# Memory keys by heads at four seams, weights split ahead of the rows, an opening and a final norm in another order

## What is computed

```
h = rmsnorm(x, norm_mix_pre[layer])
m = retention_mixer(h, ...)  or  dilated_mixer(h, ...)
x = x + rmsnorm(m, norm_mix_post[layer])
f = conv_ffn(rmsnorm(x, norm_ffn_pre[layer]), ...)
x = x + rmsnorm(f, norm_ffn_post[layer])
```

```
memn = rms_norm(mem, norm_mem)
k = (memn @ wk).reshape(B, M, MEM_HEADS, MEM_HEAD_DIM)
```

## Time and profile before

| | |
|---|---|
| median of three runs | 1215.38 us |
| the profiled execution, its own time | 1215.33 us |
| its span, first to last instruction | 1213.5 us |
| mean granted TensorE clock | 0.999 of full speed |
| busy: PE, DVE, ACT, POOL | 99%, 70%, 57%, 12% |
| HBM read | 208.08 MB, 172 GB/s over the span |
| weight splits on DVE (L2011) | 195, mean 2.19 us |
| weight splits on ACT (L1466) | 195, mean 1.84 us |

### The profile page before, as it was taken

One profiled execution on the slowest core, in us unless ns is written; L12 is line 12 of the kernel. 1 busy time (PEld: TensorE's weight loads), 2 busy tenths in 40 slices (PEclk: granted clock), 3 DMA queues, 4 the chain that ended last, 5 costly groups with the idle time before them and its releaser, 6 DMA issues.

```text
span 1213.5 us, 19309 instructions
## 1 busy us (share of the span) xinstructions
PE 1201.4 (99%) x7660; PEld 1064.7 (88%) x7660; DVE 853.7 (70%) x1235; ACT 694.6 (57%) x1014; POOL 146.5 (12%) x182
## 2 busy tenths in 40 slices
PE   8999999999999999999999999999999999999997
PEld 8888888888888889889888888888999898999896
DVE  5566665866667898888877777677666667566665
ACT  6444335665555755555555656556676567565554
POOL 1000000300001000000001311331101411001500
PEclk9999999999999999999999999999999999999999
DMA  9544434655554445444443755554354453454331
GB/s 368 213 165 173 173 139 156 220 197 195 192 189 165 174 155 169 166 161 157 159 174 122 291 201 179 201 180 173 130 201 140 139 208 110 145 188 137 134 139 53
DMA packets 31992, 210.35 MB, mean 173 GB/s; under 512 B 3665, under 2 KB 3938, under 8 KB 11042
## 3 DMA queue, kind: packets, MB, share of 16 engines
q1 hardware_dynamic: 30258, 202.12, 47.3%
q0 software_dynamic: 1504, 6.76, 1.5%
q10 hardware_dynamic: 144, 0.26, 0.1%
HBM read 208.08 MB, written 1.05 MB: 172 GB/s over the span
## 4 chain that ended last, share of the span: by engine, by line
PE 93%; DVE 3%; ACT 2%; issue 1%; DMA 1%; POOL 0%; SPq 0%; DVEq 0%; ACTq 0%; POOLq 0%
PE pair L757 18%; PE pair L639 15%; PE pair L641 15%; PE pair L640 15%; PE pair L751 10%; PE bank L639 3%; PE bank L640 3%; PE bank L641 3%; PE bank L867 1%; PE bank L1041 1%; PE pair L741 1%; PE bank L1050 1%; DVE wlo L2011 1%; PE bank L1063 1%; ACT whi L1466 1%
## 5 line engine op out<-in xcount | busy, mean ns | idle before, releaser
L2011 DVE TENSOR_TENSOR wlo<-raw,whi 128x2048 fp32r<-128x2048 f32 (+2 forms) x195 | 426.6, 2194 | 152.1 <-ACT whi L1466 151.4
L1466 ACT ACTIVATE whi<-raw 128x2048 fp32r<-128x2048 f32 (+2 forms) x195 | 357.3, 1836 | 167.7 <-PE pair L641 137.8
L757 PE MATMUL pair<-ahl,whi 128*128 128x512 f32 x832 | 208.8, 391 | 0.0
L757 PEld LDWEIGHTS pair<-ahl,whi 128*128 128x128 f32 x832 | 153.1, 188 | 29.4
L639 PE MATMUL pair<-whi,bhl 128*128 128x512 f32 (+3 forms) x416 | 150.7, 362 | 0.0
L641 PE MATMUL pair<-whi,bhl 128*128 128x512 f32 (+3 forms) x416 | 146.0, 351 | 0.0
L640 PE MATMUL pair<-wlo,bhl 128*128 128x512 f32 (+3 forms) x416 | 145.8, 351 | 0.0
L751 PE MATMUL pair<-ahl,wlo 128*128 128x256 f32 x832 | 115.2, 282 | 0.0
L751 PEld LDWEIGHTS pair<-ahl,wlo 128*128 128x128 f32 x832 | 110.5, 191 | 3.9
L639 PE MATMUL pair<-whi,ahl 128*128 128x512 f32 (+3 forms) x288 | 109.0, 379 | 0.0
L641 PE MATMUL pair<-whi,ahl 128*128 128x512 f32 (+3 forms) x288 | 106.0, 368 | 0.0
(11 more groups left out here) (338 smaller groups left out, 1967.4 us busy)
## 6 DMA issues: line engine op xcount, KB each, us to landing
raw<-wstream_d SPq DMA_DIRECT2D x161, 1024.0 KB, 4.8
raw<-wstream_d SPq DMA_DIRECT2D x26, 768.0 KB, 4.5
raw<-wstream_d SPq DMA_DIRECT2D x4, 832.0 KB, 4.9
raw<-wstream_d SPq DMA_DIRECT2D x4, 800.0 KB, 4.4
gain_row<-rows_d POOLq DMA_DIRECT2D x5, 512.0 KB, 4.1
arena<-mem_cols_d POOLq DMA_DIRECT2D x2, 1024.0 KB, 8.0
raw<-wstream_d SPq DMA_DIRECT2D x2, 576.0 KB, 4.0
raw<-wstream_d SPq DMA_DIRECT2D x2, 512.0 KB, 6.2
```

Source lines behind the costliest of these rows:

```text
L757: mm = pe.matmul(pair[:, p, f, :], whi[:, slot, sl], both, start=False, stop=k == KD - 1, skip_group_check=True)
L1466: act.activation(whi[:, n % RING, 0:width[n]], raw[:, n % RAW, 0:width[n]], ACT.Copy).then_inc(hi_ready, 1)
L2011: dve.tensor_tensor(wlo[:, n % RING, 0:width[n]], raw[:, n % RAW, 0:width[n]], whi[:, n % RING, 0:width[n]].bitcast(F32), ALU.subtract).th ...
```

## The change

1. The memory keys of layer 0 are made by heads, one head (a chunk of 128x1024, 24 matmuls) at each of the four seams, in the place of the fillers (`seam_keys`); each result is read out on its own (`read_keys`). The turn of x is cut into these keys: three k-tiles ahead of tile 0, three ahead of tile 1, two behind at seams 1 and 3; seven ahead and one behind at seams 2 and 4. The memory's rows are therefore loaded three times more and their halves made three times more, into whichever row buffer is free there; rows of x wait until the keys have been read from it (`keys_half`, `chunk_used`).
2. Splits of weights stand ahead of the squares and the weighs, or of the rows, in the lists of ACT and DVE.
3. At seams 2 and 4, whose sums lie in banks, all four weighs stand ahead of the update of tile 0.
4. In section 2, layer 0, the factors are spread one place later in the token product.
5. In the opening, the second half of chunk 0 is loaded ahead of the second half of x's columns, and chunk 1 is split in three parts.
6. The gain of the final norm is multiplied in `add_product`, ahead of its wait for PE's last sums.

```diff
-FIRST_PARTS = ((0, 512, 1024, 1536, CW), (0, 1024, CW), (0, 1024, CW))
+FIRST_PARTS = ((0, 512, 1024, 1536, CW), (0, 512, 1024, CW), (0, 1024, CW))
...
+    key_blocks = lambda l, heads: [("block", "mem_wk_2", l, np.concatenate([r(MEM_HD) + h * MEM_HD for h in heads]), r(KD))]
+    blocks += key_blocks(0, SEAM_HEADS[0:1])
...
+    blocks += key_blocks(0, SEAM_HEADS[1:2])
...
-        blocks.append(("block", "mem_wk_2", l, mem, r(KD)))
+        blocks += key_blocks(l, r(MEM_H) if l else SEAM_HEADS[3:4])
...
         mem_rows = cut(4096, NT, D)
-        mem_t = [cut(7000, KD, SEQ), cut(9400, KD, SEQ)]
+        mem_t = [cut(10000, KD, SEQ)] * 3 + [cut(7000, KD, SEQ), cut(9400, KD, SEQ)]
+        mem_rows_of = [(ahi, alo, 0), (bhi, blo, KD)] * 2 + [(bhi, blo, KD)]
...
-                    if c == 0:
-                        sp.dma_start(first_cols[:, FIRST_X[i]:FIRST_X[i + 1]], x_cols_in[:, FIRST_X[i]:FIRST_X[i + 1]]).then_inc(x_cols_sem[i], 16)
+                    if i == 0 and c < 2:
+                        sp.dma_start(first_cols[:, FIRST_X[c]:FIRST_X[c + 1]], x_cols_in[:, FIRST_X[c]:FIRST_X[c + 1]]).then_inc(x_cols_sem[c], 16)
                     sp.dma_start(raw[:, c, a:b], src[:, a:b]).then_inc(w_landed[c] if b == CW else part_in[n], 16)
...
+            pool.wait_ge(x_lo, KD // 2)
+            pool.dma_start(mem_t[0], mem_cols_in).then_inc(mem_in_sem, 16)
...
-            def keep_warm(dst, n):
-
-                for _ in range(n):
-                    pe.transpose(dst, ident[:, :], ident[:, :])
...
+            def seam_keys(seam, *cuts):
+
+                hi, lo, k0 = mem_rows_of[seam]
+                p, c = begin_block("a"), w.chunk
+                slot = c % RING
+                w.chunk += 1
+
+                def some(first, last):
+                    for k in range(first, last):
+                        if k == 0:
+                            pe.wait_ge(lo_ready, c + 1)
+                        if k % 2 == 0:
+                            pe.wait_ge(mem_lo, 4 * seam + k // 2 + 1)
+                        sl = slice(k * MEM_HD, (k + 1) * MEM_HD)
+                        mm = product(pair[:, p, 0, 0:SEQ], whi[:, slot, sl], wlo[:, slot, sl], hi[:, k0 + k, :], lo[:, k0 + k, :], k == 0, k == KD - 1)
+                        if k == KD // 2 - 1:
+                            mm.then_inc(keys_half, 1)
+                        elif k == KD - 1:
+                            mm.then_inc(chunk_used, 1)
+
+                return [lambda a=a, b=b: some(a, b) for a, b in zip((0,) + cuts, cuts + (KD,))]
+
+            def turn_rows(x_there, aside=(nothing, nothing, nothing), held=None):
 
                 base = w.at("turn")
                 for t in range(NT):
...
-                        if k == 0 and filler[t]:
-                            keep_warm(bank[:, 0, t * P:(t + 1) * P] if dst is None else dst, filler[t])
+                        if k == 0:
+                            aside[t]()
                         x_there(t, k)
...
-                if filler[2]:
-                    keep_warm(next_pair(), filler[2])
+                aside[2]()
...
-                turn_rows(added, (4, 9, 0), held=held)
+                turn_rows(added, seam_keys(2 * l, 3, 6), held)
...
-            keep_warm(aside, 18)
-            pe.wait_ge(post_ready, 2 + 4)
             held = []
-            turn_rows(added, (0, 2, 0), aside, held)
+            keys, more, rest = seam_keys(1, 7, 7)
+
+            def sums_weighed():
+                keys()
+                pe.wait_ge(post_ready, 2 + 4)
+
+            turn_rows(added, (sums_weighed, more, rest), held)
...
 
-                ready = []
-
-                def turn_first():
-                    if l == 0:
+                if l == 0:
+                    keys, more, rest = seam_keys(3, 7, 7)
+
+                    def sums_weighed():
+                        keys()
                         pe.wait_ge(post_ready, 2 * (2 + 4))
-                    ready.append(turn_rows(summed if l else added))
-
-                rows_there = lambda a, b: pe.wait_ge(mem_lo, 4 * l + b // 2)
-                features("a", bhi, blo, k0=KD, lhs_ready=rows_there, between=[nothing, nothing, turn_first])
-                ready = ready[0]
-                tokens("v", ahi, alo, lhs_ready=ready, between=[spread_rows])
+
+                    ready = turn_rows(added, (sums_weighed, more, rest))
+                    tokens("v", ahi, alo, lhs_ready=ready, between=[nothing, nothing, spread_rows])
+                else:
+                    ready = []
+                    rows_there = lambda a, b: pe.wait_ge(mem_lo, 4 * 4 + b // 2)
+                    features("a", bhi, blo, k0=KD, lhs_ready=rows_there, between=[nothing, nothing, lambda: ready.append(turn_rows(summed))])
+                    ready = ready[0]
+                    tokens("v", ahi, alo, lhs_ready=ready, between=[spread_rows])
...
+            def rows_out(dst, gain, each=False, classes=False, keys=None):
                 for g in range(KD // 2):
+                    if keys is not None and g == 0:
+                        act.wait_ge(keys_half, keys + 1)
+                    elif keys is not None and g == KD // 4:
+                        act.wait_ge(chunk_used, w.chunk + 1)
...
             def ffn(l):
-                split_hi(w.chunk - 2)
-                rows_out([(ahi, 0)], [COLS["norm_ffn_pre"] + l * KD], True)
+                catch_up()
+                rows_out([(ahi, 0)], [COLS["norm_ffn_pre"] + l * KD], True, keys=2 * l)
+                passed()
+                read_keys(2 * l)
...
+                    if i == FF_TILES - 1:
+                        catch_up()
...
-                row_squares(added if l == 0 else summed)
-
-                catch_up()
-                passed()
+                if l:
+                    row_squares(summed)
+                    catch_up()
+                    passed()
...
+                else:
+                    p, n = read_keys(3)
+                    row_squares(added)
...
+                if not in_pairs:
+                    weigh(1, 0)
+                    weigh(1, 1)
                 dve.wait_ge(post_ready, half_done[0])
                 dve.wait_ge(*done[0])
                 dve.wait_ge(rstd_ready, w.up("rstd"))
                 dve.scalar_tensor_tensor(x[:, 0, :], xn[:, 0, :], rstd[:, 0:1], x[:, 0, :], ALU.mult, ALU.add).then_inc(x_ready, 1)
-                weigh(1, 0)
-                weigh(1, 1)
+                if in_pairs:
+                    weigh(1, 0)
+                    weigh(1, 1)
...
                 dve.tensor_tensor(xh[:, 1, 0, :], xh[:, 1, 0, :], pair[:, p, 0, :], ALU.add).then_inc(x_half, 1)
+                if meanwhile is not None:
+                    meanwhile()
                 w.chunk += 1
                 dve.wait_ge(chunk_used, w.chunk)
                 dve.tensor_tensor(xh[:, 1, 1, :], xh[:, 1, 1, :], pair[:, p, 1, :], ALU.add).then_inc(drained_v[p], 1)
...
+            def final_gain():
+
+                dve.wait_ge(gain_in, 16 * w.up("gain"))
+                dve.wait_ge(x_half, 4 * 3 + 2 * DEPTH)
+                dve.tensor_tensor(xn[:, 1, 0:D // 2], x[:, 1, 0:D // 2], gain_row[:, 0:D // 2], ALU.mult).then_inc(gained, 1)
+
...
+            mem_low(0, 0)
             used(1)
             ret_norm(RET_HEADS - 1, g_at[RET_HEADS - 1])
-            used(2)
+            mem_low(0, 1)
+            used(1)
+            mem_low(0, 2)
+            used(1)
             ret_out(RET_HEADS - 1)
+            mem_low(0, 3)
             used(RET_KT // 2 - 6)
-            passed()
+            used(1)
             add_post(in_pairs=True)
...
+                passed()
+                w.next_block("a")
...
+                    if i >= FF_TILES - KD and i % 2 == 0:
+                        mem_low(2 * l + 1, KD // 2 - (FF_TILES - i) // 2)
...
+            mem_low(2, 0)
+            mem_low(2, 1)
             dil_weigh(c, 1)
...
+            mem_low(2, 2)
+            mem_low(2, 3)
             split_lo(w.chunk - 2)
             dil_osplit(c)
+            catch_up()
             add_post(in_pairs=True)
```

92 lines of the change are left out of this document (53 added, 39 removed).

## The result

Five runs of the change gave 1208.79 to 1209.77 us, median **1209.43**; five of the kernel before 1215.3 to 1215.55, median 1215.35. The ratio is 0.995, 95% interval 0.9939 to 0.996. The forecast was 1209.5.

The account below looks back on a forecast made before the run. PE, busy 99% of the span, was taken to bound the kernel. The terms -1.1 + 1.4 - 0.1 + 1.3 - 7.1 - 0.3 = -5.9 took 1215.33 to 1209.5 us, range 1207.2 to 1213.0.

Parts of the forecast that it names:

- Seam 1: Retention to the first FFN: the up product starts 1.4 us later, with 2.88 of key matmuls inside.
- Seam 2: First FFN to attention: the up product starts 0.1 us sooner, with 2.88 of key matmuls inside.
- Seam 3: Attention to the second FFN: the up product starts 1.3 us later, with 2.88 of key matmuls inside.
- Seam 4: Second FFN to section 2: tokens start 7.1 us sooner, with 8.6 less key work inside and 1.5 of new waiting.
- Tail: End of the kernel: the final gain's product moves into DVE's wait for PE, and 0.3 us reaches the store.
- Signs: If right: next product 5.1 to 5.2 us after PE is free at Seam 1 and Seam 2; DVE wait 1 to 2 at Seam 4.
- Opening: Start of the kernel: PE's two waits for split weights, at 10.60 and 14.44, go; gain 1.1 us.
- The first: Rival at Seam 4: ACT and DVE are quicker and PE loses nothing there; 1208.0 us, chance 0.12.
- The second: Rival at four seams: POOL is held by splits and weighs, each row factor 0.9 us late; 1213.1, chance 0.08.
- The third: Rival behind the seams: weights are split late, a miss of 0.9 us at three seams; 1212.2, chance 0.12.
- The fourth: Rival: DVE's chain sets each seam anyway and keys only fill it; 1213.7 to 1214.5 us, chance 0.07.
- The fifth: Rival at Seam 4 and Seam 2: without fillers TensorE's clock falls; 1218 us and more, chance 0.05.

Follow-up runs that it names:

- experiment 6: The change with DVE's split of the up chunk moved behind tile 0's update at the seams from retention and attention to the FFNs: 1212.18 us.
- experiment 4: The change with tile 1's weighs put back behind tile 0's update, at the seams after the first and second FFN: 1209.17 us.
- experiment 5: The change with the product of the final norm's gain put back behind the last sums: 1210.07 us.
- experiment 3: The kernel before without its 46 filler transposes: 1216.27 us; with only the fillers between first FFN and attention kept: 1215.42 us.
- experiments 2: The change with 14 pairs of warm-up transposes in place of 11: 1209.1 us; the change itself once more: 1209.79 us.
- experiment 7: The change with the token product's first two steps, after the second FFN, doing high-half matmuls before waiting for low halves: 1210.43 us.

## Why the prediction was right, and where it was not

*Seam 1: right, step by step.* The forecast had ACT's split from 199.3 (199.54 measured), DVE's split done at 203.8 (203.85), the weighs done at 205.1 (205.05), tile 0 turned from 206.4 (206.49), the up product at 209.9 (209.87). Part of that is luck: 199.3, 1.9 and 2.29 add up to 203.5, and the 203.8 of the forecast holds 0.3 that it names no row for; ACT began 0.24 late. One bound, "without DVE's delay it would be 209.15", can't be had by moving the split: experiment 6 took it out of the weighs' way and the seam got 1.22 longer. I had looked at what is late for tile 0; the seam ends with tile 1, behind the sum of DVE's work.

*Seam 2: 0.28 sooner, not 0.1.* The chain of the last weigh, x and the turn held (PE waits 0.28, not 0.6). That weighs go first had no part in it, by experiment 4.

*Seam 3: right* (1.36 for 1.3), seam 1 repeated.

*Seam 4: right* (7.08 for 7.1). Of its 6.16, 24 keys take 2.88 and 16 transposes some 1.76; the other 1.5 are the new waiting that was worked out, and the rows name 0.28 of it for x and 0.93 for DVE's low rows.

*Tail: right,* 0.34 for 0.3, and experiment 5 gives back 0.33.

*Signs.* Two of the signs set ahead were just missed: seam 2 took 4.89 and not 5.1 to 5.2, and the wait on DVE at seam 4 was 0.93 and not 1 to 2.

*Opening: this step failed,* the 1.1 of the sum. Its two waits did go, but the pitch of 0.12 on which I valued them was read from one execution. The matmuls of the opening run at 0.21 in others, and with the old order nobody sees it, since PE waits for weights anyway: the kernel before with the slow pace (experiment 3, first profile) reaches the first 512-column matmul at 20.28, with the quick pace at 20.30. The order of the opening removes a wait that hid a slow clock. At the quick pace it is worth 1.36 to 1.45 there and 0.9 to 1.4 at the end (experiments 2, 4 and 5), so the 1.1 was a fair price for that pace; at the slow pace it is worth nothing. The median of five runs holds some of both.

*What made the sum come out:* the FFNs' first up matmuls wait less for high rows (0.12 and 0.14), and section 2 lost 0.33, of which 0.31 lies in one place in its second layer. Before, DVE stands idle for 0.85 ahead of its L2349 at 1109.15, ended by "issue" (nothing that the profile shows), runs 0.3 to 0.4 late from there on, and PE's L1272 at 1121.89, which needs DVE's result (L2353), starts 0.31 late. In the change DVE's idle time at that place (1103.94) is 0.50, and PE starts without a stop. It is 0.50 too in the profile of the opening alone, whose code there is that of before, and 0.85 and 0.84 in the two with fewer fillers. What makes it 0.85 or 0.50 is not shown; it was not tried. So 0.3 of the gain belongs to no part of the change that was thought of. (The sum as written, 1215.33 - 5.9, is 1209.43; the forecast has 1209.5.)

*Rivals.* The first (seam 4 stays covered) is refuted by the 0.93 and 0.28. The second was right that POOL would be held by a split of DVE, while its condition for a price, that the weighs hold it as well, did not come: POOL's L543, 0.32 at seam 1 before, took 0.99 and 0.96 at seams 1 and 3, ending 0.19 behind DVE's split, while the weighs still ran, as the forecast said; in experiment 7 a POOL row held by splits did cost time. The Trainium skill, page "SBUF — State Buffer", section "SBUF: two separate sides", has a DVE operation with two SBUF inputs keep a reading GpSimd operation out for its whole length; the rows of 0.99, 0.96 and 2.01 agree. The third (weights late) did not come: no wait for a split within 10 us behind a seam. The fourth (1213.7 to 1214.5) is refuted by the time. The fifth did not come either, but I set it aside with a wrong reason. I read a clock of 1.00 through stretches where PE did little as a sign that the fillers were of no use to it; experiment 3 shows that 2.8 us without them bring 0.50. In the change keys have taken the fillers' place, PE's longest wait in a seam is 0.93, and the granted clock is 1.00 behind all four seams.

## What to carry to other kernels

Work that is needed later and depends on inputs alone is the best filler there is: spread over the places where the critical engine waits, 72 matmuls left the last seam for waits at three others, and the fillers went with them, provided that every place keeps enough of it to hold the clock. A wait that is removed in the first microseconds may have hidden a slow clock, so value it by several profiles and not by one. And where one engine is sped up, look for small operations of another that lived in a gap which now closes; here moving the consumer by one place was enough.
